# Hybrid decoder step: second weight loads issued by GpSimd, joint sums two slots sooner, the last batch's smaller sums on TensorE

## What is computed

```python
def mixer_layer(x, l, lw, past, past_len, win_buf):
    h = rms_norm(x, norm_g)
    proj = jnp.einsum('btd,dn->btn', h, w_in)
    ...
    oa = diff_attention(qa, kv_a[:, :, 0]..., kv_a[:, :, 1], q_pos, jnp.arange(L), lam)
    oa = rms_norm(oa, a_out_g) * (1.0 - lam_init)
    ya = oa.reshape(B, T, D_A) * jax.nn.silu(az.astype(f32))
    ...
    ob = g[..., 0:1] * o_cs[..., 0, :] + g[..., 1:2] * o_cs[..., 1, :] + g[..., 2:3] * o_win
    yb = ob.reshape(B, T, D_B) * jax.nn.silu(bz.astype(f32))
    ...
    hc = rms_norm(hc, c_out_g) * jax.nn.sigmoid(co.astype(f32).reshape(B, T, H_C, DV_C))
    yc = hc.reshape(B, T, D_C) * jax.nn.silu(cz.astype(f32))
    mix = jnp.concatenate([ya, yb, yc], axis=-1)
    y = x + jnp.einsum('btm,md->btd', mix, w_out.astype(f32)).astype(x.dtype)
```

## Time and profile before

| | |
|---|---|
| median of 3 runs (lowest, highest) | 1845.36 us (1841.63, 1846.11) |
| the profiled execution, its own time | 1846.04 us |
| its span, first to last instruction | 1844.3 us |
| TensorE busy | 1635.2 us (89%) |
| VectorE, ScalarE, GpSimd busy | 794.3, 610.6, 120.9 us |
| decode stage, output stage | 1043 to 1564 us, 1565 to 1844 us |
| mean granted clock of TensorE, of full speed | 0.944 |

### The profile page before, as it was taken

The page is one execution under the profiler, slowest core; times in us unless marked ns, Lnnn a source line. Parts: engine busy times, 40 slices in busy tenths (PEclk is TensorE's granted clock), DMA queues, the critical chain, the costliest instruction groups (busy, mean ns, idle before and its releaser), DMA issues. The chain is left out here.

```text
span 1844.3 us, 39009 instructions
## 1 busy us (share of the span) xinstructions
PE 1635.2 (89%) x14817; PEld 1267.5 (69%) x14817; DVE 794.3 (43%) x1567; ACT 610.6 (33%) x1397; POOL 120.9 (7%) x186
## 2 busy tenths in 40 slices
PE   6999999998998899998968788989898986698787
PEld 5888888886777667776656666667666664576566
DVE  4212121263257444433535445666556556743121
ACT  4311111232122222221225255555555556421110
POOL 3000000062000001000022000000000001100000
PEclk8999999999999999999987699999999999798898
DMA  6555555685332325255245579999998998632453
GB/s 202 175 183 187 185 184 167 204 289 191 116 107 93 116 87 153 83 132 178 76 152 210 196 269 382 344 346 347 366 331 324 376 340 306 234 103 81 127 184 106
DMA packets 221863, 379.57 MB, mean 206 GB/s; under 512 B 42325, under 2 KB 122758, under 8 KB 220366
## 3 DMA queue, kind: packets, MB, share of 16 engines
q1 hardware_dynamic: 217566, 363.97, 58.3%
q0 software_dynamic: 3824, 11.02, 1.7%
q10 hardware_dynamic: 288, 2.10, 0.3%
HBM read 340.57 MB, written 40.71 MB: 207 GB/s over the span
## 5 line engine op out<-in xcount | busy, mean ns | idle before, releaser
L378 PE MATMUL pj_ps<-pj_whi,pj_xhi 128*128 128x512 f32 (+1 forms) x1024 | 415.3, 406 | 6.1 <-PEq L95 6.0
L379 PE MATMUL pj_ps<-pj_wlo,pj_xhi 128*128 128x512 f32 (+1 forms) x1024 | 400.3, 391 | 0.0
L380 PE MATMUL pj_ps<-pj_whi,pj_xlo 128*128 128x512 f32 (+1 forms) x1024 | 399.2, 390 | 0.0
L296 DVE TENSOR_TENSOR pj_wlo<-pj_w,pj_whi 128x1024 fp32r<-128x1024 f32 (+1 forms) x128 | 154.8, 1210 | 449.0 <-ACT pj_whi L254 447.5
L254 ACT ACTIVATE pj_whi<-pj_w 128x1024 fp32r<-128x1024 f32 (+1 forms) x128 | 132.3, 1033 | 508.8 <-DMA pj_w<-in_w_in 508.7
L378 PEld LDWEIGHTS pj_ps<-pj_whi,pj_xhi 128*128 128x128 f32 x1024 | 196.6, 192 | 66.8 <-issue 30.5
L380 PEld LDWEIGHTS pj_ps<-pj_whi,pj_xlo 128*128 128x128 f32 x1024 | 196.9, 192 | 40.4
L379 PEld LDWEIGHTS pj_ps<-pj_wlo,pj_xhi 128*128 128x128 f32 x1024 | 197.2, 193 | 34.0
L1871 ACT ACTIVATE fr_kT<-da_tp 128x512 f32<-128x512 f32 x200 | 119.4, 597 | 167.8 <-PE da_tp L1753 164.5
L1978 DVE COPY fr_kT<-da_tp 128x512 f32<-128x512 f32 x128 | 88.3, 690 | 93.0 <-PE da_tp L1753 92.7
L1753 PE MATMUL da_tp<-all_ident,fr_front 128*128 128x128 f32 x640 | 93.5, 285 | 23.8 <-DMA fr_front<-in_cache_a_kv 16.1
(11 more groups left out here) (554 smaller groups left out, 2162.4 us busy)
## 6 DMA issues: line engine op xcount, KB each, us to landing
fr_front<-in_cache_a_kv SPq DMA_DIRECT2D x128, 512.0 KB, 6.4
da_pa<-in_cache_a_kv SPq DMA_DIRECT2D x128, 512.0 KB, 6.3
pj_w<-in_w_in SPq DMA_DIRECT2D x120, 512.0 KB, 4.6
px_pages<-in_cache_b_kv SPq DMA_DIRECT2D x256, 128.0 KB, 2.5
fr_front<-in_cache_b_kv SPq DMA_DIRECT2D x128, 128.0 KB, 6.4
da_pb<-in_cache_b_kv SPq DMA_DIRECT2D x128, 128.0 KB, 6.3
proj<-pj_out SPq DMA_DIRECT2D x52, 256.0 KB, 4.9
fr_kT<-in_w_out SPq DMA_DIRECT2D x16, 512.0 KB, 4.3
```

The lines of the kernel that those rows point to most:

```text
L296: dve.tensor_tensor(self.wlo[:, r, :, 0:n], self.w[:, r, :, 0:n], self.whi[:, r, :, 0:n], ALU.subtract).then_inc(self.wlo_ready, 1)
L378: pe.matmul(acc, hi, high, start=kc == 0, stop=False)
L379: pe.matmul(acc, hi, low, start=False, stop=False)
L380: last = pe.matmul(acc, lo, high, start=False, stop=kc == KC - 1)
```

## The change

Three things change, all near the end of the kernel.

1. `load_again` leaves SyncE's list. GpSimd issues the 16 second loads, behind its last `weigh`: the first two wait for `att_stored`, the others for the use of the buffer. GpSimd also gets a wait for `mixed` ahead of its gating of tile 1.
2. The joint sums' steps stand one or two slots sooner on VectorE, ScalarE and TensorE; `store_attended` and the load of `LAST` go from g = 13 and 14 to g = 11 in SyncE's list; the squares of `LAST` stand behind `high_w(16)`.
3. For the last batch VectorE does only the reduction into `oa`. TensorE forms the other two sums as products with the unit matrix, 9 and 2 accumulating ones, and ScalarE copies them to `os` between the squares and the root of tile 0.

```diff
@@ decode_attend, TensorE
                 for _ in tiles:
                     pass
+                pe.wait_ge(last_weighed, 1)
+                for x, (c0, c1) in enumerate(((S0, W0), (W0, NC))):
+                    for c in range(c0, c1):
+                        last = pe.matmul(go[:, x, :], k.ident[:], ob[:, (DB - 1) % 2, c, :], start=c == c0, stop=c == c1 - 1)
+                last.then_inc(last_summed, 1)
@@ decode_attend, ScalarE
                 out.square_a(act, 0, 1, HA, sa)
+                act.wait_ge(last_summed, 1)
+                act.activation(os_[:, :, DB - 1, :], go[:, 0:2, :], ACT.Copy)
                 out.root(act, 0)
@@ decode_attend, VectorE, finish
                         if part == 3 and b == DB - 1:
-                            dve.wait_ge(last_weighed, 1)
                             return
...
-                    else:
+                    elif part == 4 or b < DB - 1:
@@ Output.run, SyncE
-                    def load_again(x):
-                        j, c = divmod(x, NP)
-                        if x >= 2:
-                            sp.wait_ge(wx_used, x - 1)
-                        sp.dma_start(wx[x % 2], self.wv[:, PC * c:PC * c + PC, SLAB * j:SLAB * j + SLAB]).then_inc(
-                            wx_loaded[x % 2], 16)
...
-                            if g == NP + 5:
+                            if g == NP + 3:
                                 store_attended()
-                            if g == NP + 6:
                                 sp.wait_ge(att_stored, 16 * 3 * HA)
                                 load_tile(LAST)
...
-                                load_again(0)
-                                load_again(1)
-                            if g > LATE and g - LATE + 1 < LATE:
-                                load_again(g - LATE + 1)
@@ Output.run, GpSimd
+                    pool.wait_ge(mixed, 1)
                     for u in range(1, len(TURN)):
                         self.weigh(pool, u)
+                    for x in range(LATE):
+                        j, c = divmod(x, NP)
+                        if x < 2:
+                            pool.wait_ge(att_stored, 16 * 3 * HA)
+                        else:
+                            pool.wait_ge(wx_used, x - 1)
+                        pool.dma_start(wx[x % 2], self.wv[:, PC * c:PC * c + PC, SLAB * j:SLAB * j + SLAB]).then_inc(
+                            wx_loaded[x % 2], 16)
@@ Output.run, ScalarE
-                        if g == NP + 3:
+                        if g == NP + 2:
                             act.wait_ge(j_centred, 1)
...
-                        if g == NP + 6:
+                        if g == NP + 4:
                             copy_out(2)
-                        if g == NP + 7:
+                        if g == LATE:
                             self.square_c(act, LAST, 0, HC, ps[PT])
@@ Output.run, VectorE
-                        if g == NP + 1:
+                        if g == NP:
                             join_maxima()
                             join_sums()
+                        if g == NP + 1:
+                            scale_parts()
                         if g == NP + 2:
-                            scale_parts()
-                        if g == NP + 4:
                             for x in range(3, 6):
                                 copy_out(x)
@@ Output.run, TensorE
+                                if g == NP + 1 and t == 2:
+                                    pe.wait_ge(j_shared, 1)
+                                    pe.transpose(tp[0][:, 2 * P:2 * P + 2 * DB], joint[:, 3, :],
+                                                 k.ident[0:2 * DB, 0:2 * DB]).then_inc(j_back, 1)
                                 multiply(j, c, t)
...
                             if g == NP + 2:
-                                pe.wait_ge(j_shared, 1)
-                                pe.transpose(tp[0][:, 2 * P:2 * P + 2 * DB], joint[:, 3, :],
-                                             k.ident[0:2 * DB, 0:2 * DB]).then_inc(j_back, 1)
-                            if g == NP + 4:
                                 pe.wait_ge(j_ready, 2)
```

More of the change, by code:

```diff
@@ L1684, in decode_attend @@
         last_weighed = s.sem("last_weighed")
+        last_summed = s.sem("last_summed")
         at = {(b, what, p): n for n, (b, what, p) in enumerate(steps)}
```

## The result

| | before | after |
|---|---|---|
| median of runs (lowest, highest) | 1845.7 us (1841.6, 1846.1) | 1817.1 us (1813.2, 1822.7) |
| span of the profiled execution | 1844.3 us | 1815.6 us |
| mean granted clock of TensorE | 0.944 | 0.951 |
| ratio after / before, 95% interval | | 0.985 [0.982, 0.988] |

The changed kernel is faster by 28.6 us; 1818.5 was forecast.

A forecast was written before the change was run, and what follows sets the result against it. TensorE, busy 89% of the span, was taken as the bound, its idle and lower-clock time as winnable. Terms +3.7 - 7.1 - 12.5 - 11.2 = -27.1 took 1846.04 us to 1818.9, stated as 1818.5; 8-in-10 range 1811 to 1828.

The forecast's parts named there:

- decode stage's end: End of decode: ScalarE waits for TensorE's 22 records ahead of table load, root and squares; 4.5 us longer, other end 2.4.
- less on `mix_a(0)`: Output stage's start: GpSimd's gatings no longer slow `mix_a(0)`; of 2.06 us gained 0.8 stays, bounds 0 and 2.06.
- start of the output stage: Net of the longer decode stage and the gain on `mix_a(0)`: +3.7 us, bounds +0.4 and +4.9.
- slot 16: wait: TensorE's 8.7 us wait for `add_x` shrinks to 2.8 as the last tile loads sooner: -5.9, bounds -7.7 and -2.0.
- slot 16: restart: Lower-clock restart behind the `add_x` wait, 2.48 us now: may come or not, half taken, -1.2.
- second loads: Slots 18 and 26: on GpSimd's queue both TensorE waits for `kept` slabs go whole with restarts, -12.5 and -11.2 us.
- The choice of the lower clock: Decode stage's end: TensorE's 22 records take 0.21 us each, 4.9 in all, as granted clock is 0.50 by then.
- the other bound (2.4): Decode stage's end: at the upper clock the 22 records take 2.9 us and the stage gets only 2.4 longer.
- Rival 2: Decode end is cheap: sums at upper clock, all 2.06 kept, start costs 0.4 instead of 3.7; 1815 us, chance 0.10.
- Rival 1: Slot 16's wait stays near 8 us with restart, w(16) or last tile landing 5 later; 1825.5 us, chance 0.13.
- Rivals 3 and 4: GpSimd's loads late: beside the stores, 11 us more, 1829.5, chance 0.04; or everywhere, slower, 1854 at latency 18, chance 0.03.
- The gatings: GpSimd's gatings of tile 1 would move from `mix_a(0)` onto `low_w(0)` and `mix_b(0)`; 0.8 of 2.06 us stays.

The follow-up runs named there:

- e10: Changed kernel with 16 more unit-matrix products on TensorE, never read, ahead of the last batch's sums: 1812.6 us, ratio 0.983.
- e3: Kernel before with only the joint sums' steps, their stores, the last tile's load and squares moved; second loads stay on SyncE: 1836.1 us, ratio 0.996.
- e5: Changed kernel with the second loads back on SyncE, each ahead of its slot's `load_w` and stores: 1825.0 us, ratio 0.992.
- e9: Changed kernel, TensorE taking only the window's sum, first root ahead of the copy, tile 1's squares later, `LAST`'s squares and `mix(LAST)` sooner: 1803.2 us, ratio 0.979.
- e1: Changed kernel with VectorE's three reductions for the last batch again, no sums on TensorE and no copy: 1811.5 us, ratio 0.983.
- e6: Changed kernel with ScalarE's wait for the sums and its copy moved behind the root and tile 1's squares: 1807.7 us, ratio 0.982.
- e7: Changed kernel without GpSimd's wait for `mixed`: 1810.6 us, ratio 0.986.
- e8: Changed kernel with GpSimd's second loads (from x = 2) waiting also for the next slot's product: 1817.5 us, ratio 0.988.
- e4: Kernel before with only the last batch's two smaller sums on TensorE and ScalarE's copy of them: 1843.6 us, ratio 1.000.
- e2: Kernel before with only the second loads moved to GpSimd's queue, no wait for `mixed`: 1818.8 us, ratio 0.987.

## Why the prediction was right, term by term

| term | forecast | measured, after against before |
|---|---|---|
| decode stage's end | +4.5 (2.4 to 4.9) | +4.50 (first `high_w`) |
| less on `mix_a(0)` | -0.8 (0 to 2.06) | -1.03 (first `high_w` to first product) |
| start of the output stage | +3.7 | +3.47 (first product) |
| slots 0 to 15 without the wait | none | -0.83 |
| slot 16: wait | -5.9 (-7.7 to -2.0) | -6.3 |
| slot 16: restart | -1.2 (0 to -2.48) | -0.7 (end of the wait to first sample product: 10.14, now 9.43) |
| second loads | -12.5 and -11.2 | -12.53 and -11.29 |
| slot 17 | none | +1.57 |
| sum | -27.1 | -26.57 |

The waits came as forecast. That the sum is right to 0.5 us is luck in its small parts. Restart and slot 17 together are 2.1 worse than forecast. Most of it is made up for by 0.8 in slots 0 to 7, which no step of the change explains, 0.4 at the wait and 0.2 at the start.

- **The decode stage's end.** Right in mechanism and size, 22 records at 0.22 each. The choice of the lower clock rested on one window at 1559.3 us in the earlier trace rows; e10 shows that the other bound (2.4) was as real. Rival 2 needed the upper clock and all of the 2.06; neither came. VectorE's three reductions were not equal thirds: the one that is left takes 2.12 of the 4.42, so VectorE lost 2.3 and not 2.9, which changes nothing, as it was not the last engine.
- **Slot 16.** The chain came as it was laid out: `load_w(16)` issued at 1676.44 (forecast 1675.6), `high_w(16)` done at 1682.2 (1682), root at 1687.4 (1687.2), TensorE's start at 1694.79 (1694.6). The two scales can be laid on each other here, since slot 8 starts at 1641.76 in before and 1642.29 in after; that they lie so close is chance. Rival 1 needed w(16) some 5 us later. The nearest to it are e3 and e5, with two second loads ahead of w(16): `high_w(16)` came 3.4 and 2.8 us later behind the first product than in after, and the `add_x` waits were 5.1 and 5.2. That this term was safe only together with the first part was in the working (GpSimd takes the first two second loads too) but not said; e3 and e5 show it.
- **The restart.** From its first product to slot 17's, slot 16 takes 8.71 us in e9, which has no wait, 11.15 in before and 10.50 in after. So 8.66 us of waiting cost 2.44 of restart, and 2.40 of waiting still cost 1.79 (1.70 to 1.74 in e1, e6, e7, e8 and e10, with waits of 1.9 to 2.4). The prediction took half of 2.48 as the expected value of a fall or none; the restart came each time, and the term was 0.5 too good.
- **The second loads.** Both waits went whole, with their restarts. But after the first sample products TensorE's clock fell once more:

```profile
1704.00:1708.00 4.00, 3.77 (x38) 2.99 (x39) 2.36 (x2) 2.07 (x3) 0.72 (x1) 0.64 0.46 133
```

  The slot from 1704.23 took 8.25 us instead of 6.68. The same slot takes 6.68 to 6.70 in before, e1, e3, e4, e6, e7, e9 and e10, and 8.25 to 8.30 in after, e2, e5 and e8. The prediction had no term for it.
- **Rivals 3 and 4** rested on GpSimd's landing. It is 3.9 to 9.2 with a median of 5.7, next to 3.8 to 8.2 in the earlier trace rows; the loads that ran beside a TensorE that never pauses took at most 7.3, and 12.4 would have been in time. The SBUF port of which the Trainium skill warns (SBUF — State Buffer, SBUF: two separate sides) delayed nothing here that could be measured.
- **The gatings.** In before GpSimd's gatings start first (1565.60) and keep 3.14 us, and `mix_a(0)`, which starts at 1565.95, pays 2.06. In after `low_w(0)` starts first, at 1569.40, and keeps its 1.22, and GpSimd, which starts at 1569.56, pays:

```profile
1569.56 1.96 POOL L3154 TENSOR_TENSOR fr_front<-fr_front,fr_bg 128x512 f32<-128x512 f32 x1 [17.34 <-DVE fr_front L3409]
```

  This first gating takes 1.96 instead of 1.04. Its second takes 1.04 and costs `mix_b(0)`'s first operation 0.30, that costs the third 0.4 (1.49 for 1.09), and the third costs `mix_b(0)`'s second operation 0.73: the loss changes hands each time. `low(0, 0)`, which reads PSUM, took 0.75 in both kernels, in after beside GpSimd. The prediction had `low_w(0)` hit; it was GpSimd that waited. The Trainium skill (SBUF — State Buffer, SBUF: two separate sides) says just that of two instructions that contend: the one that starts first has the shared port for its whole time, and the other one is blocked. The rows agree; the prediction drew only on who contends and not on who comes first.

## What to carry to other kernels

When a load waits both for its buffer and for its turn in a queue of stores, give it a queue that nothing else waits in; the one place further ahead in the same queue that was tried brought only part. Before work is handed to an idle engine, look at who has to wait for it and what stands behind that wait: here the same sums cost 4.5 us with ScalarE's wait ahead of its root and squares, and 0.6 with it behind them. And TensorE, idle for 3.96 us before, did the handed work at 1.2 GHz: 4.91 us instead of 2.72. A wait that is shortened and not removed keeps most of its restart: 1.8 us behind a wait of 2.4, 2.4 behind one of 8.7. Part measurements of a few microseconds in 1840 are decided on the traces, laid side by side at a shared event, since the times of e4 alone would have hidden a real 4.5 us; and figures near 1 us are not decided even there by one trace of each kernel.

## What was not expected of the hardware

- TensorE's clock fell after small gaps at slots 16 and 17: in after 2.40 us of idleness were followed by 0.67 between 1695 and 1700 us, and a gap of 0.99, together with the short transpositions of `LAST`, by 0.64 between 1704 and 1708. With the same 0.99 and no wait before it e9 shows 1.00 there. But e1, e6, e7 and e10 had a wait for `add_x` of 1.9 to 2.4 too, before, e3 and e4 one of 5.1 to 8.7, and their slot 17 kept 6.68 to 6.70. What decides between these cases the traces don't show, and it was not settled.
- Which of two contending instructions pays depends on which starts first, by tenths of a microsecond: in after `low_w(0)` led by 0.16 us and lost nothing, and GpSimd's first gating lost 0.92; in before GpSimd led by 0.35 and lost nothing, and `mix_a(0)` lost 2.06. So moving a start by little can move a loss of 1 to 2 us from one engine to another. Here part of it went to GpSimd, whose result was not yet wanted.
- Issuing a transfer occupies GpSimd for 0.72 us, SyncE for 0.43; neither mattered, as GpSimd has nothing else to do there.
